# Exchanging the halves of q and k for the rotary rotation: products with a matrix, or DMAs within SBUF

## The reference, cut to what matters

```python
def rotary(x, pos):
    half = x.shape[-1] // 2
    inv = ROPE_THETA ** (-jnp.arange(half, dtype=jnp.float32) / half)
    ang = pos.astype(jnp.float32)[:, None] * inv[None, :]
    cos, sin = jnp.cos(ang)[None, :, None, :], jnp.sin(ang)[None, :, None, :]
    x1, x2 = x[..., :half], x[..., half:]
    return jnp.concatenate([x1 * cos - x2 * sin, x2 * cos + x1 * sin], axis=-1)
...
h = rms_norm(x, odd_norm_g[j])
qkv = (h @ odd_w_qkv[j]).reshape(bn, s, 3, ATTN_HEADS, HEAD_DIM)
q, k, v = rotary(qkv[:, :, 0], pos), rotary(qkv[:, :, 1], pos), qkv[:, :, 2]
```

## Time and profile before

| | before |
|---|---|
| three runs, median (lowest to highest) | 1676.9 us (1675.8 to 1677.26) |
| the profiled execution, its own time | 1676.46 us |
| its span, first to last instruction | 1674.7 us |
| mean granted TensorE clock | 0.968 |
| TensorE matmuls busy | 1555.6 us (93%) |
| VectorE, ScalarE, GpSimd busy | 691.7, 511.4, 117.7 us |
| DMA moved | 375.72 MB, 224 GB/s over the span |

### The profile page before, as it was taken

One profiled execution on the slowest core, in us unless ns is written; L12 is line 12 of the kernel. 1 busy time (PEld: TensorE's weight loads), 2 busy tenths in 40 slices (PEclk: granted clock), 3 DMA queues, 4 the chain that ended last, 5 costly groups with the idle time before them and its releaser, 6 DMA issues.

```text
span 1674.7 us, 26947 instructions
## 1 busy us (share of the span) xinstructions
PE 1555.6 (93%) x10672; PEld 1269.1 (76%) x10672; DVE 691.7 (41%) x1296; ACT 511.4 (31%) x831; POOL 117.7 (7%) x50
## 2 busy tenths in 40 slices
PE   7988999989998999989998887998899999999997
PEld 5767999989678999978887876887666655555554
DVE  5945888357566886232414421412311111111111
ACT  2355554354446564352223104202111101111100
POOL 0111122212001122100000000000000000000000
PEclk9989999999999999989999987999799999999999
DMA  7664555745434656514442211354799999999994
GB/s 298 235 261 164 168 168 165 254 137 166 146 115 125 188 182 184 161 50 146 131 126 76 64 38 50 105 155 139 298 428 426 427 428 426 428 425 428 427 427 208
DMA packets 57977, 375.72 MB, mean 224 GB/s; under 512 B 6560, under 2 KB 6816, under 8 KB 42272
## 3 DMA queue, kind: packets, MB, share of 16 engines
q1 hardware_dynamic: 57888, 374.43, 60.6%
HBM read 373.35 MB, written 1.05 MB: 224 GB/s over the span
## 4 chain that ended last, share of the span: by engine, by line
PE 62%; DMA 15%; issue 12%; DVE 6%; ACT 3%; POOL 0%; SPq 0%; POOLq 0%; DVEq 0%; ACTq 0%
PE lin L617 15%; DMA moe_arena<-in_experts 14%; PE lin L598 5%; PE mixp L1145 4%; PE lin L599 4%; PE lin L600 4%; PE mixp L1149 4%; DVE mixers L1700 3%; PE lin L901 2%; PE stat L1169 2%; PE lin L1124 1%; PE stat L598 1%; PE mixp L600 1%; PE mixp L598 1%; PE stat L600 1%
## 5 line engine op out<-in xcount | busy, mean ns | idle before, releaser
L598 PE MATMUL lin<-r_hi,w_hi 128*128 128x256 f32 x1024 | 301.4, 294 | 16.8 <-DVE r_lo L1571 8.9
L599 PE MATMUL lin<-r_lo,w_hi 128*128 128x256 f32 x1024 | 293.7, 287 | 0.0
L600 PE MATMUL lin<-r_hi,w_lo 128*128 128x256 f32 x1024 | 293.6, 287 | 0.0
L617 PE MATMUL lin<-h,ring 128*128 128x256 f32 x1280 | 288.0, 385 | 3.0 <-DVE h L1583 3.0
L617 PEld LDWEIGHTS lin<-h,ring 128*128 128x128 f32 x1280 | 245.8, 193 | 40.7 <-issue 6.9
L598 PEld LDWEIGHTS lin<-r_hi,w_hi 128*128 128x128 f32 x1024 | 200.3, 196 | 22.9 <-issue 9.6
L599 PEld LDWEIGHTS lin<-r_lo,w_hi 128*128 128x128 f32 x1024 | 200.9, 196 | 0.7
L600 PEld LDWEIGHTS lin<-r_hi,w_lo 128*128 128x128 f32 x1024 | 200.5, 196 | 0.0
L1559 DVE TENSOR_TENSOR w_lo<-ring,w_hi 128x1024 fp32r<-128x1024 f32 x126 | 156.0, 1242 | 93.6 <-ACT w_hi L1216 70.1
L2175 DVE TENSOR_TENSOR moe_arena<-moe_arena,mixp 128x256 f32<-128x256 f32 x32 | 13.5, 421 | 353.3 <-ACT moe_arena L1505 353.3
L1216 ACT ACTIVATE w_hi<-ring 128x1024 fp32r<-128x1024 f32 x124 | 130.0, 1050 | 59.8 <-PE mixp L600 54.5
(11 more groups left out here) (378 smaller groups left out, 2332.3 us busy)
## 6 DMA issues: line engine op xcount, KB each, us to landing
moe_arena<-in_experts SPq DMA_DIRECT2D x96, 2048.0 KB, 18.5
ring<-in_panels SPq DMA_DIRECT2D x272, 512.0 KB, 3.6
aring<-in_ada SPq DMA_DIRECT2D x24, 1024.0 KB, 6.3
cst<-in_consts SPq DMA_DIRECT2D x1, 1696.0 KB, 11.7
x<-in_x SPq DMA_DIRECT2D x1, 1024.0 KB, 4.7
out_x<-x SPq DMA_DIRECT2D x2, 512.0 KB, 2.6
mixers<-in_even_w_s SPq DMA_DIRECT2D x1, 512.0 KB, 13.4
colp<-in_cols SPq DMA_DIRECT2D x1, 361.5 KB, 5.1
```

The lines of the kernel that those rows point to most:

```text
L598: pe.matmul(o, w_hi[:, slot, c], r[0], start=start, stop=False, skip_group_check=True)
L599: pe.matmul(o, w_hi[:, slot, c], r[1], start=False, stop=False, skip_group_check=True)
L600: return pe.matmul(o, w_lo[:, slot, c], r[0], start=False, stop=stop, skip_group_check=True)
L617: mm = pe.matmul(lin[b][:, 0:T], w[:, i, :], rhs[:, i, :], start=i == 0, stop=i == k - 1)
```

## The change

The product with the permutation matrix is taken off TensorE. For each of the 16 q and k panels SP issues four DMAs, each of 32 partitions of 1 KB, from `qs1` to a new buffer `qw1`; the sign that the matrix held goes into the sines. `qs1` and `qw1` have four buffers each. SP's loads in this stage are written out one by one between the exchanges: load of panel n+4, exchange of panel n (behind a wait for its eviction and, from the third on, for the finished rotation of panel n-2), load of panel n+5, and so on. `K["swap"]` goes (128 of the constants' columns). The diff:

```diff
@@ -108,12 +108,6 @@
     d = np.arange(P) % HD
     inv = (10000.0 ** (-np.arange(HD // 2, dtype=np.float32) / np.float32(HD // 2))).astype(np.float32)
     ang = (np.arange(T, dtype=np.float32)[None, :] * inv[d % 32][:, None]).astype(np.float32)
-    swap = np.zeros((P, P), np.float32)
-    for p in range(P):
-        if p % HD < 32:
-            swap[p + 32, p] = -1.0
-        else:
-            swap[p - 32, p] = 1.0
 
     def pattern_bias(q0, k0):
         q = q0 + np.arange(P)[:, None]
@@ -127,7 +121,7 @@
         "eps": np.full((P, 1), EPS), "one": np.ones((P, 1)), "ones": np.ones((P, P)),
         "ident": j == t, "mean512": np.full((P, P), 1.0 / HALF),
         "upto": j <= t, "before": j < t, "after": j > t,
-        "cos": np.cos(ang), "sin": np.sin(ang), "swap": swap,
+        "cos": np.cos(ang), "sin": np.where(d[:, None] % HD < 32, -np.sin(ang), np.sin(ang)),
         "bias00": pattern_bias(0, 0), "bias10": pattern_bias(P, 0), "bias11": pattern_bias(P, P),
         "neg_causal": np.where(j <= t, 0.0, NEG),
         "upto64": (j <= t) & same, "ones64": same, "neg_causal64": np.where((j <= t) & same, 0.0, NEG),
@@ -278,7 +272,7 @@
         yb_normed = sem("yb_normed")
         yb_ready = sem("yb_ready")
 
-        rot_ready = sem("rot_ready")
+        halves_swapped = [sem(f"halves_swapped{b}") for b in range(2)]
         qk_ready = sem("qk_ready")
         vt1_ready = sem("vt1_ready")
         vt1_copied = sem("vt1_copied")
@@ -419,11 +413,12 @@
 
         a = Arena(mixers_t, MIXERS)
         qk1 = a.take(16 * T).rearrange("p (k t) -> p k t", k=16)
-        qs1 = a.take(2 * T).rearrange("p (k t) -> p k t", k=2)
         rc1 = a.take(2 * T).rearrange("p (k t) -> p k t", k=2)
         v1 = a.take(8 * T).rearrange("p (k t) -> p k t", k=8)
         vt1 = a.take(NT * D).rearrange("p (c f) -> p c f", c=NT)
         SC = 3 * P
+        qs1, qw1 = (mixers_t[:, a.at + i * RING * T:a.at + (i + 1) * RING * T].rearrange("p (k t) -> p k t", k=RING)
+                    for i in range(2))
         s1 = a.take(4 * SC).rearrange("p (b s) -> p b s", b=4)
         p1 = a.take(4 * SC).rearrange("p (b s) -> p b s", b=4)
         pt1 = a.take(4 * SC).rearrange("p (b s) -> p b s", b=4)
@@ -522,15 +517,31 @@
 
             load_ffn(2)
             load_ada(3)
-            load_panels(3 * KD)
+            panels_seen.advance(LN_PANELS + KD + 2 * KF)
+            panels_seen.advance_down()
+            load_panels(4)
+
+            def swap_halves(n):
+
+                panels_seen.advance(1)
+                b = (panels_seen.n - 1) % RING
+                sp.wait_ge(bank_free[b], panels_seen.free[b])
+                if n >= 2:
+                    sp.wait_ge(qk_ready, n - 1)
+                for o in (0, 64):
+                    for to, at in ((o, o + 32), (o + 32, o)):
+                        sp.dma_start(qw1[to:to + 32, n % RING, :], qs1[at:at + 32, n % RING, :]).then_inc(halves_swapped[n % 2], 16)
+
+            for n in range(16):
+                load_panels(1)
+                swap_halves(n)
+            load_panels(4)
             load_panels(4)
             load_ada(5)
             load_panels(KD - 4)
             load_ffn()
             load_panels(PANELS - BLOCK2)
-            panels_seen.advance(LN_PANELS + KD + 2 * KF)
-            panels_seen.advance_down()
-            panels_seen.advance(3 * KD)
+            panels_seen.advance(KD)
             panels_seen.advance(KD + 2 * KF)
             panels_seen.advance_down()
             panels_seen.advance(PANELS - BLOCK2)
@@ -790,22 +801,9 @@
             ffn(True)
 
 
-            def swap_halves(n):
-
-                b = (qk_first + n) % 4
-                pe.wait_ge(bank_free[b], panels.free[b])
-                if n >= 2:
-                    pe.wait_ge(qk_ready, n - 1)
-                pe.matmul(stat[:, 2 * (n % 2), :], K["swap"], qs1[:, n % 2, :], start=True, stop=True)\
-                    .then_inc(rot_ready, 1)
-
-            qk_first = panels.n
-            for n in range(16):
-                linear(None, 1, first=n == 0)
-                if n:
-                    swap_halves(n - 1)
+            linear(None, 1, first=True)
+            linear(None, 15)
             linear(None, 1)
-            swap_halves(15)
             linear(None, 7)
             panels.settled()
             for g in range(4):
@@ -1338,9 +1336,9 @@
 
             stream_norm(down=True)
             for n in range(16):
-                if n >= 2:
-                    act.wait_ge(qk_ready, n - 1)
-                take(qs1[:, n % 2, :])
+                if n >= RING:
+                    act.wait_ge(qk_ready, n - RING + 1)
+                take(qs1[:, n % RING, :])
             for n in range(8):
                 take(v1[:, n, :])
             for i in range(HEADS + 2):
@@ -1756,9 +1754,9 @@
             for n in range(16):
                 panels.taken(0)
                 panels.advance(1)
-                link(dve.tensor_tensor(rc1[:, 0, :], qs1[:, n % 2, :], K["cos"], ALU.mult))
-                dve.wait_ge(rot_ready, n + 1)
-                link(dve.tensor_tensor(rc1[:, 1, :], stat[:, 2 * (n % 2), :], K["sin"], ALU.mult))
+                link(dve.tensor_tensor(rc1[:, 0, :], qs1[:, n % RING, :], K["cos"], ALU.mult))
+                dve.wait_ge(halves_swapped[n % 2], 64 * (n // 2 + 1))
+                link(dve.tensor_tensor(rc1[:, 1, :], qw1[:, n % RING, :], K["sin"], ALU.mult))
                 dve.tensor_tensor(qk1[:, n, :], rc1[:, 0, :], rc1[:, 1, :], ALU.add).then_inc(qk_ready, 1)
                 dve.wait_ge(qk_ready, n + 1)
                 split_lo(panels.n + 4)
```

## The result

| | before | changed |
|---|---|---|
| runs, median (lowest to highest) | 1677.08 us (1675.04 to 1679.81, 6) | 1685.76 us (1684.18 to 1688.04, 6) |
| ratio to before, 95% interval | | 1.0052 (1.0039 to 1.0065) |
| profiled execution, its span | 1674.7 us | 1682.1 us |
| stage: from the start of panel 0's eviction to that of panel 23's | 72.94 us | 84.25 us |

The change costs 8.7 us. The forecast was 4.2 us gained, 1672.7 us, with a range up to 1679.5. It moved by 11.3 us, the span by 7.4 and the median by 8.7. I judge mechanisms by the stage: parts that the change doesn't touch differ by some us between executions (in the eleven profiles of this study, panel 0's eviction starts anywhere from 357.2 to 363.9 us).

What follows compares the result with a forecast made beforehand. TensorE was taken to bound the q and k stage: 6.7 us gained by removing its exchanges, less 2.5 us lost waiting behind late loads, makes 4.2 us; 1676.9 - 4.2 = 1672.7 us, range 1669.4 to 1679.5.

Steps and rivals of the forecast that it cites:

- the gain from TensorE: q and k panels: TensorE bounds the stage; removing 16 exchanges of 0.42 us each makes 6.7 us.
- the loads' loop: Eviction, four SP issues, load, rounding, eviction two panels on: 6.34 us, 3.17 a panel against TensorE's 2.88; TensorE loses 2.5 us.
- and nowhere before 12: Sign of being right: TensorE waits for the rest parts of panels near 17, and for none before panel 12.
- The stock of four panels: TensorE's lead of four panels, which the slower loop over evictions and loads was to eat before TensorE waits near panel 17.
- the issue on SP: Four exchange issues a panel on SP, 0.33 us each and up to 0.43 back to back; 1.31 us in the loop.
- 3.6 and 0.15: In the loop, a panel load lands 3.6 us after its issue; 0.15 us added for uncertain landing, making 1.0 us of waiting.
- My own rule for it: TensorE's wait near panel 17: 1.5 us, plus 0.7 us for each 0.1 us more in the 6.34 us loop.
- Rival 3: Longer loop, 7.5 to 7.7 us, from issues of 0.43 and landings of 4.4 to 4.6: 1680.1 to 1681.2 us; chance 0.22.
- The landing of an exchange: A 32 KB transfer within SBUF lands 2.0 us after its issue, with 1.4 and 3.6 as ends.
- The exchange's round trip: DVE's rest part of panel n+4 behind the exchange wait: 5.5 us, to 7.1, against 8.6 available; this wait alone covered.
- rival 4: Exchange n waits for the rotation of n-2, 4.0 of 5.8 us; decides only from a 4 us landing; no chance of its own.
- Rival 2: DVE becomes the bound, pacing at 3.15 us a panel; gain about 2 us, time 1675, no change; chance 0.10.

Runs made afterwards that it cites:

- in pairs: Changed kernel with four DMAs per two panels, loads six ahead two at a time, both rest parts before both rotations on DVE: 1672.04 us, ratio 0.9973.

## Why the prediction was wrong

**The bound, the gain from TensorE: right.** 6.7 us was forecast for taking the exchanges off; with one DMA a panel the stage fell by 7.2 us, in pairs by 6.05.

**The mechanism of the loss: right.** It was the loads' loop, with its places in order, and the chain of waits shows it piece by piece. The evictions of alternate panels hang on one another, and ScalarE is released by the loads. Its effect came earlier than forecast: TensorE was to wait near panel 17 "and nowhere before 12", and it first waits at 373.1 us, ahead of panel 6, 0.54 us for a rest part. The stock of four panels goes sooner in a loop of 8.5 us than in one of 6.34.

**The step that failed is the size of a term: the issue on SP.** I wrote "an issue costs SP 0.33 us and up to 0.43 back to back". These are the rows of loads from HBM. An exchange's issue took 0.59 us: 2.45 us for four, not 1.31. The load behind them was the second error: 4.5 us on the chain, from its issue to landing, in place of 3.6 and 0.15 (its own issue is 0.25 us longer, the rest I didn't take apart). Together the loop was 8.5 us, not 6.5. My own rule for it, 1.5 us of TensorE's waits and 0.7 for each 0.1 us over 6.34, then gives 1.5 + 7 x 2.16 = 16.6 us: 72.9 - 6.7 + 16.6 = 82.8 us of stage, measured 84.25. The arithmetic was sound and its input was not.

**The range had no room for it.** Rival 3 put 0.43 us as the dearest issue, the dearest of the panel loads; the experts' loads had one of 0.76 us, which I passed over. And no row showed an issue within SBUF at all. I had bounded the landing of an exchange from both sides and taken the issue as known. The loop multiplies each issue by 4 x 7, so it was the number to bound most widely. At 0.6 us an issue and with rival 3's landings (+0.8 to 1.0) the same formula gives 1.5 + 7 x 1.9 = 14.8 us of waits and 1685.0 us, up to 1686.4, beyond rival 3's slow end of 1681.2. The issue alone, with the forecast's own 3.6 and 0.15 us for the load, gives 1680.4: just beyond the range and 5.4 us short of the measured time. So both terms are in the miss. The range's upper end, 1679.5, is also 0.6 below the 1680.1 that rival 3 works out as its near end; either is far short of 1685.8.

**The landing of an exchange**, 2.0 us (1.4 to 3.6) forecast, was 2.4 at the median and 1.8 to 3.5. The Trainium skill (DMA: Bandwidth & Descriptors, rules for kernel authors) says to join transfers below 64 KB. I let it change nothing, since I weighed it by landings only; and the 2.1 us worked out in the prediction uses a fixed cost that the page's section on the anatomy of a DMA gives for DMAs issued by GpSimd, where SP issues these. The runs agree with the rule, through the issues: with nothing else changed, two DMAs of 64 KB a panel in place of four of 32 KB bring the stage from 84.3 to 72.7 us.

**The exchange's round trip** stands in the prediction twice. As the path over the rotation to the rest part that TensorE needs, it was called covered ("This wait alone is covered"). It is covered only while the loads' loop is the slower one: with the loads five ahead, taking the rest part out from behind the rotation gave 5.5 us of stage. I had left out SP's dearer issues and the GpSimd part that holds a rotation for 2 us. As rival 4, the wait of exchange n for the rotation of n-2, it got no chance, and in the changed kernel SP never has that wait. With five ahead it appears:

```profile
SPq L530 <- DVE mixers L1760: 4.7, 4, 1.5
```

What those 4.7 us cost the stage no run shows.

**Rival 2**, DVE as the bound, didn't come: with the waits in the right place 47.4 us of work fit into 66.9.

## What to carry to other kernels

Replacing an instruction on the critical engine by DMAs moves its price to the issuing queue: count issues times their duration there, and follow who waits for what stands behind them in that queue. When a transfer of a new kind enters a loop, bound its issue time as widely as its landing, and multiply by how often the loop goes round. Before such a replacement is judged, put prefetches ahead of it in the queue, put what the bound engine needs before the wait, and join transfers; here the three together turned 8.7 us lost into 4.9 us gained.

## What was not expected of the hardware

- Issuing a DMA from SBUF to SBUF on SyncE took 0.47 us with the queue idle for one of 128 partitions, 0.51 for 32, and 0.59 us back to back, for 16, 32 and 64 partitions and for 1 or 2 KB a row. A load from HBM took 0.33 us alone and 0.58 behind such a DMA.
- A few issues took far longer (up to 1.88 us, with the loads six ahead), in most of the kernels with exchanges; nothing in the trace says why.
- A sum of two SBUF operands on DVE, like the cosine product of before, was held for 2.5 us while GpSimd made a rest part, and so was the sine product, which now reads SBUF (2.37 us in the chain above). The Trainium skill (SBUF — State Buffer, two separate sides) calls this an exclusive lock; the trace agrees for all three. The sum, from DVE's timeline, beside GpSimd's rest part, from its own, in the changed kernel:

```profile
383.99 2.59 DVE L1760 TENSOR_TENSOR mixers<-mixers 128x256 f32<-128x256 f32 x1
...
383.89 2.41 POOL L1528 TENSOR_TENSOR w_lo<-ring,w_hi 128x1024 fp32r<-128x1024 f32 x1 [14.52 <-ACT w_hi L1208]
```
